# First expert's prompt rows by a selection product instead of a gather, its first low part on GpSimd, and two moved steps in attention

## The reference, cut to what matters

```
h2 = rms_norm(x, norm2_g)
aff = softmax(h2 @ w_router)                 # tokens x 16
gates, idx = top_k(aff.T, cap)               # each expert picks its tokens: 32 of the prompt, 64 of the sample
xe = h2[idx]
ye = (silu(xe @ w_gate) * (xe @ w_up)) @ w_down
x[idx] += ye * gates
```

## Time and profile before

| | us |
|---|---|
| median of 3 runs (1507.14 to 1507.4) | 1507.22 |
| the profiled execution, its own time | 1507.2 |
| its span | 1505.4 |
| TensorE busy | 1481.9 (98%) |
| VectorE busy | 1246.6 (83%) |
| ScalarE busy | 1115.2 (74%) |
| GpSimd busy | 285.9 (19%) |

### The profile page before, as it was taken

One profiled execution on the slowest core, in us unless ns is written; L12 is line 12 of the kernel. 1 busy time (PEld: TensorE's weight loads), 2 busy tenths in 40 slices (PEclk: granted clock), 3 DMA queues, 4 the chain that ended last, 5 costly groups with the idle time before them and its releaser, 6 DMA issues.

```text
span 1505.4 us, 18866 instructions
## 1 busy us (share of the span) xinstructions
PE 1481.9 (98%) x7283; PEld 1212.8 (81%) x7283; DVE 1246.6 (83%) x1237; ACT 1115.2 (74%) x1354; POOL 285.9 (19%) x115
## 2 busy tenths in 40 slices
PE   7999999999999999999999999999999999999997
PEld 6788887677778888888888888888888888888886
DVE  5358688875898989898988989898988989898985
ACT  7556476866487878878787878878787878878784
POOL 1012020000110404132240404132240404131010
PEclk9999999999999999999999999999999999999999
DMA  6111112204699999999999999999999999999993
GB/s 238 57 56 57 57 34 79 87 1 152 251 350 396 374 393 376 388 380 386 382 377 392 376 393 374 388 381 387 383 373 391 376 393 376 388 383 387 393 380 107
DMA packets 192105, 447.47 MB, mean 297 GB/s; under 512 B 13257, under 2 KB 13585, under 8 KB 192017
## 3 DMA queue, kind: packets, MB, share of 16 engines
q1 hardware_dynamic: 187632, 433.56, 77.4%
q0 software_dynamic: 4224, 12.65, 3.7%
q10 hardware_dynamic: 160, 0.07, 0.0%
HBM read 433.66 MB, written 12.58 MB: 296 GB/s over the span
## 4 chain that ended last, share of the span: by engine, by line
PE 95%; ACT 2%; DVE 2%; DMA 0%; issue 0%; POOLq 0%; POOL 0%; DVEq 0%; ACTq 0%
PE ps L1044 23%; PE ps L1046 23%; PE ps L1045 23%; PE ps L658 6%; PE ps L660 5%; PE ps L659 5%; PE ps L1108 1%; PE ps L896 1%; PE ps L932 1%; PE ps L1029 1%; PE ps L916 1%; ACT wih L1166 0%; PE ps L771 0%; ACT yr L1226 0%; PE ps L766 0%
## 5 line engine op out<-in xcount | busy, mean ns | idle before, releaser
L2039 DVE TENSOR_TENSOR wl<-raw,wh 128x2048 fp32r<-128x2048 f32 x384 | 872.1, 2289 | 114.7 <-ACT wh L1495 112.5
L1495 ACT CAST wh<-raw 128x2048 fp32r<-128x2048 f32 x384 | 729.7, 1915 | 117.5 <-PE ps L1046 116.2
L1044 PE MATMUL ps<-wh,XTh 128*128 128x512 f32 x1016 | 401.8, 395 | 0.6 <-DVE wl L2039 0.6
L1046 PE MATMUL ps<-wl,XTh 128*128 128x512 f32 x1016 | 396.3, 390 | 0.0
L1045 PE MATMUL ps<-wh,XTl 128*128 128x512 f32 x1016 | 395.4, 389 | 0.0
L1046 PEld LDWEIGHTS ps<-wl,XTh 128*128 128x128 f32 x1016 | 190.7, 188 | 40.9
L1044 PEld LDWEIGHTS ps<-wh,XTh 128*128 128x128 f32 x1016 | 190.8, 188 | 38.4 <-DVE wl L2039 1.0
L1045 PEld LDWEIGHTS ps<-wh,XTl 128*128 128x128 f32 x1016 | 191.0, 188 | 37.8
L1044 PE MATMUL ps<-wh,gTh 128*128 128x512 f32 x512 | 200.9, 392 | 0.0
L1046 PE MATMUL ps<-wl,gTh 128*128 128x512 f32 x512 | 199.4, 390 | 0.0
L1045 PE MATMUL ps<-wh,gTl 128*128 128x512 f32 x512 | 199.2, 389 | 0.0
(11 more groups left out here) (277 smaller groups left out, 1625.5 us busy)
## 6 DMA issues: line engine op xcount, KB each, us to landing
raw<-in_w_gate SPq DMA_DIRECT2D x128, 1024.0 KB, 11.2
raw<-in_w_up SPq DMA_DIRECT2D x128, 1024.0 KB, 11.2
raw<-in_w_down SPq DMA_DIRECT2D x128, 1024.0 KB, 11.5
slice_raw<-in_w_in SPq DMA_DIRECT2D x5, 2048.0 KB, 7.8
X<-in_x_sample SPq DMA_DIRECT2D x8, 512.0 KB, 6.5
slice_raw<-in_w_out SPq DMA_DIRECT2D x2, 2048.0 KB, 8.3
X<-in_x_prompt SPq DMA_DIRECT2D x4, 512.0 KB, 7.1
slice_raw<-in_w_in SPq DMA_DIRECT2D x4, 512.0 KB, 7.5
```

The lines of the kernel that those rows point to most:

```text
L1044: pe.matmul(out, hi, rhs_h, start=first, stop=False)
L1046: return pe.matmul(out, hi, rhs_l, start=False, stop=last)
L1495: act.copy(wh[:, n % CONV, :], raw[:, n % RAW, :]).then_inc(s_wh, 1)
L2039: dve.tensor_tensor(wl[:, n % CONV, :], raw[:, n % RAW, :], wh[:, n % CONV, :].bitcast(F32), ALU.subtract).then_inc(s_wl, 1)
```

## The change

In the attention loop, ScalarE's copy of the last value unit is done at step 4 instead of step 5, and from step 24 on TensorE's fillers come ahead of the transposes of mixed weights, as in the steps before.

Between router and first expert, the first expert's prompt rows are no longer gathered. VectorE writes the indices as numbers (`idxf`); TensorE multiplies them by a matrix with one row of ones (`pick`), which spreads the first expert's 32 indices over all partitions; VectorE compares them with each partition's token number (`token`, a new small input) and scales by the token's root (`onehot`, two tiles of 128 by 32); TensorE multiplies the residual rows `X` by that, two products for each of eight feature blocks, into the PSUM columns beside the turned sample rows. The sample rows alone are turned earlier, between the rounds. The fourth pair of feature blocks is done inside the first weight tile, whose order of products changes. The low part of weight tile 0 moves from VectorE to GpSimd, behind the gather of the sample rows. The copy of the candidates moves ahead of the second half of the prompt's softmax, and the sample's gates move behind the first of the four rounds. TensorE's busy-work is shortened.

```diff
+            sp.dma_start(token[:], a["token_index"]).then_inc(s_wr, 16)
...
             gather_sample(0)
+            pool.wait_ge(s_wh, 1)
+            pool.tensor_tensor(wl[:, 0, :], raw[:, 0, :], wh[:, 0, :].bitcast(F32), ALU.subtract).then_inc(s_wl, 1)
...
             pool.wait_ge(s_route, 2)
-            gather_prompt(0)
-            pool.memset(nlam[:, 1:2], 0.0).then_inc(s_issued, 1)
             gather(1)
...
-                if i < len(ATT):
-                    for x in FILL.get(i, ()):
-                        fill(x)
+                for x in FILL.get(i, ()):
+                    fill(x)
...
-                if i >= len(ATT):
-                    for x in FILL.get(i, ()):
-                        fill(x)
...
-                keep_busy(6)
+                keep_busy(6 if r < 3 else 3)
+            pe.wait_ge(s_gat, 16)
+            for k in range(KD):
+                pe.transpose(ps[:, pair_bank(k // 2), (k % 2) * CAP:(k % 2) * CAP + CAP_S],
+                             XE[0:CAP_S, k * P:(k + 1) * P], ident[0:CAP_S, 0:CAP_S])
             pe.wait_ge(s_top, (CAP_S + CAP_P) // 8)
-            keep_busy(14)
-            pe.wait_ge(s_tables, 1)
+            keep_busy(2)
+            pe.wait_ge(s_onehot, 1)
+            pe.matmul(ps[:, 2, 2 * P:2 * P + CAP_P], pick[0:GR, :], idxf[0:GR, :], start=True, stop=True).then_inc(s_topT, 1)
+            keep_busy(1)
+
+            def first_prompt_rows(j):
+                for k in (2 * j, 2 * j + 1):
+                    for t in range(2):
+                        mm = pe.matmul(ps[:, pair_bank(j), (k % 2) * CAP + CAP_S:(k % 2 + 1) * CAP],
+                                       X[:, t, k * P:(k + 1) * P], onehot[:, t, :], start=(t == 0), stop=(t == 1),
+                                       skip_group_check=True)
+                mm.then_inc(s_xtp0, 1)
...
-                    pe.wait_ge(s_wl, n + 1)
-                    for k in range(4):
...
+                    pe.wait_ge(s_wh, n + 1)
+                    for j in range(2):
+                        pe.wait_ge(s_xth0, j + 1)
+                        for k in (2 * j, 2 * j + 1):
+                            pe.matmul(out, XTh[0][:, k, :], h_[:, k, :], start=(k == 0), stop=False)
+                        if j == 0:
+                            first_prompt_rows(3)
+                        pe.wait_ge(s_xtl0, j + 1)
+                        for k in (2 * j, 2 * j + 1):
+                            pe.matmul(out, XTl[0][:, k, :], h_[:, k, :], start=False, stop=False)
+                    pe.wait_ge(s_wl, n + 1)
                     for k in range(4):
+                        mm = pe.matmul(out, XTh[0][:, k, :], l_[:, k, :], start=False, stop=False)
...
-            turn_first_rows()
-            pe.wait_ge(s_pad, 3)
+            pe.wait_ge(s_tables, 1)
+            pe.wait_ge(s_onehot, 3)
+            for j in range(3):
+                first_prompt_rows(j)
+            pe.wait_ge(s_pad, 2)
...
-                if i in (2, 5):
+                if i in (2, 4):
                     copy_unit("tok", len(SLICES) - 1, ORDER[4] if i == 2 else ORDER[5])
...
+            dve.wait_ge(s_topT, 1)
+            ch.mark(dve.tensor_copy(cand[0:CAP_S, :], ps[0:CAP_S, 3, 0:P]))
             affinity_scaled(prompt, stat_of[:, :, 2], 2)
...
-            dve.wait_ge(s_topT, 1)
-            ch.link(dve.tensor_copy(cand[0:n, :], ps[0:n, 3, 0:P]))
...
-            ch.mark(dve.tensor_tensor(gate[0:n, 0:NE], val[0:n, first], val[0:n, second], ALU.max))
...
                 top_eight(rest, c, ps[rest, 2, 0:2 * P] if c == 0 else aff[rest, :], CAP_S // 8 + c // 8 + 1, c + 8 < CAP_P)
+                if c == 0:
+                    ch.mark(dve.tensor_tensor(gate[0:n, 0:NE], val[0:n, first], val[0:n, second], ALU.max))
+            dve.tensor_copy(idxf[0:GR, :], topi[0:GR, 0:CAP_P]).then_inc(s_onehot, 1)
             dve.transpose(pidx[0:CAP_P, :], topi[rest, 0:CAP_P]).then_inc(s_route, 1)
             dve.transpose(gate[rest, :], topv[rest, 0:CAP_P]).then_inc(s_tables, 1)
+            dve.wait_ge(s_topT, 2)
+            for t in range(2):
+                dve.tensor_scalar(onehot[:, t, :], ps[:, 2, 2 * P:2 * P + CAP_P], token[:, t:t + 1],
+                                  roots2[:, root_place(t):root_place(t) + 1], ALU.is_equal, ALU.mult).then_inc(s_onehot, 1)
...
-            dve.wait_ge(s_issued, 1)
-            split(0)
             xt_first_copy()
+            dve.wait_ge(s_wl, 1)
             for n in range(1, AHEAD):
```

More of the change, by code:

```diff
@@ L262, in build @@
         cand = at("cand", 211360, [P, 2 * CAP_S])
+        pick = at("pick", 211872, [P, P])
+        onehot = at("onehot", 212384, [P, 2, CAP_P])
+        idxf = at("idxf", 212640, [P, CAP_P])
+        token = at("token", 212896, [P, 2])
         wout_low = slice_low
@@ L329, in build @@
         s_pad = sem("spare_columns_cleared")
-        s_issued = sem("first_gather_issued")
+        s_onehot = sem("first_prompt_indices_cast_then_one_hot_rows")
         s_tables = sem("gates_and_output_rows_ready")
@@ L587, in gather @@
                 if e == 1:
-                    pool.wait_ge(s_xtp0, 4)
+                    pool.wait_ge(s_xtp0, 1)
                 else:
@@ L1016, in _ @@
                 pe.wait_ge(s_top, CAP_S // 8 + r)
-                keep_busy(6)
-            pe.wait_ge(s_top, (CAP_S + CAP_P) // 8)
-            keep_busy(14)
-            pe.wait_ge(s_tables, 1)
+                keep_busy(6 if r < 3 else 3)
[3 more added lines that the diff above has]
+                             XE[0:CAP_S, k * P:(k + 1) * P], ident[0:CAP_S, 0:CAP_S])
+            pe.wait_ge(s_top, (CAP_S + CAP_P) // 8)
+            keep_busy(2)
[9 more added lines that the diff above has]
+                mm.then_inc(s_xtp0, 1)
             def turn_rows(e, half):
                 if half == 0:
-                    pe.wait_ge(s_gat, 32 * (e + 1))
+                    pe.wait_ge(s_gat, 32 * e + 16)
                 else:
@@ L1031, in turn_rows @@
                 mm.then_inc(s_xtp, 1)
[L1033 to L1039, removed]
             def products(out, parts, rhs_h, rhs_l, first, last):
@@ L1125, in _ @@
                 turns = q % NS == 1 and e + 1 < NE
+                if q == NS:
+                    pe.wait_ge(s_pad, 3)
                 if e >= 1 and q % NS == 0:
@@ L1869, in beside @@
                 if i == 13:
-                    dve.wait_ge(s_wr, 32)
+                    dve.wait_ge(s_wr, 48)
                     dve.memset(wr[:, :, NE:32], 0.0).then_inc(s_wrg, 1)
@@ L1927, in _ @@
             dve.memset(afft[:], 0.0).then_inc(s_clear, 1)
+            ch.mark(dve.memset(pick[0:GR, :], 0.0))
             dve.memset(tabf[:, 128:256], 0.0).then_inc(s_clear, 1)
@@ L1955, in _ @@
             h2_copied(2)
+            ch.own()
+            ch.mark(dve.memset(pick[CAP_S:CAP_S + 1, :], 1.0))
             gla_turned_low(1)
@@ L2115, in shape_constants @@
     return {"ident": np.eye(P, dtype=f), "rot": np.ascontiguousarray(rot), "scan_mask": scan,
-            "pair_mask": mask}
+            "pair_mask": mask, "token_index": np.arange(2 * P, dtype=f).reshape(2, P).T.copy()}
 def kernel(**inputs):
```

## The result

The changed kernel takes **1515.07 us** (median of 5 runs, 1514.04 to 1516.02) against 1507.4 (1507.14 to 1508.02) for the kernel before, run beside it: 1.005 times as long, 95% interval 1.0039 to 1.0061. So it is 7.7 us slower, where 1505.9 was forecast with a range up to 1507.9. The profiled execution is the longest of the five: 1516.02 us, span 1514.2.

A forecast was written before the change was run, and what follows sets the result against it. TensorE was taken as the bound (95% of the chain), so only its waits count: 1.3 and 0.2 gained in attention, 0.2 lost before the third tile, 1.3 off 1507.2, giving 1505.9 us, range 1504.4 to 1507.9.

The forecast's parts named there:

- Attention: Attention steps 4 and 24 to 26: shorter TensorE waits for ScalarE's copies save 1.3 and 0.2 us.
- The rounds: Prompt's search rounds: first starts at 404.23 instead of 404.62, second at 405.94; last search ends 0.2 us earlier.
- GpSimd's price: Weight tile 0's low part on GpSimd: 4.5 us, between 4.5 and 6.6, costing TensorE nothing.
- The margin: After the first round: VectorE's gates' operation starts 0.15 us before GpSimd's subtraction, in the same order each time.
- the rival: GpSimd starts before the gates' operation and holds VectorE until 410.4; 1509.9 us, or 1512.0; chance 13%.
- The hold: After the rounds: GpSimd holds VectorE's index cast until 410.5; bounds nothing and 0.55 us.
- From first maxima to prompt rows: Router stage: first round starts at 404.23, TensorE starts on the prompt rows at 411.45.
- 0.9 a pair: Prompt-row products on TensorE: each pair of feature blocks takes 0.9 us, three pairs lasting until 414.15.
- dear end of 1.5 a pair: Prompt-row products: upper bound of 1.5 us per pair, if weight loads don't overlap.
- VectorE's low part stays last: Before the third weight tile: TensorE's wait still ends on VectorE's low part; tile starts at 421.3, 0.2 us lost.
- The removed gather: First expert's prompt rows: product replaces gather, so TensorE starts on them at 411.45 instead of 413.63.

The follow-up runs named there:

- e2: The kernel before with only the two changed orders in attention (value copy at step 4, fillers first late on); 1506.15 us against 1507.32.
- e1: The changed kernel with more TensorE busy-work between the rounds and the prompt rows, filling its waits; 1512.18 us against 1507.32 for the kernel before.
- e5: e1 plus one busy-work product after each feature block of the first three pairs, the fourth pair's two blocks set apart; 1511.91 us.
- e6: e1 plus two busy-work products after each feature block of the first three pairs, the fourth pair's two blocks set apart; 1512.63 us.
- e7: The changed kernel with a 64th indirect transfer, a gather whose rows nobody uses; 1510.78 us against 1507.26 for the kernel before.
- e9: The kernel before, gather kept, plus attention orders, moved copy and gates, half of tile 0's low part on GpSimd, tile 1's low part earlier; 1505.42 us.
- e10: e1 with the gates' operation one round later, so that it falls into GpSimd's subtraction; 1517.52 us, one run.
- e3: The kernel before with only its TensorE busy-work shortened, in the last round and behind the rounds; 1508.34 us against 1507.32.
- e4: e1 with GpSimd's subtraction held back until the cast of the indices is done; 1511.69 us against 1507.32 for the kernel before.
- e12: The changed kernel with half the low part on GpSimd, waits filled, third and fourth pairs inside the first tile, low parts reordered, 64 transfers; 1505.43 us.
- e13: e9 with the gates' operation moved behind the transpose of the indices; 1504.84 us against 1507.3 for the kernel before.
- e14: e12 with the gates' operation behind the transpose of the indices and one busy-work product less behind the third round; 1505.77 us.

## Why the prediction was wrong, point by point

- **Attention: right in mechanism, 0.3 short.** 1.3 + 0.2 was forecast. `wT` is late next, as written (0.28 before L920), and the two waits shrink by 1.5, but in e2, with attention alone, 1.2 arrives at the first maxima.
- **The rounds: right.** From first to second maxima 1.72 us (406.20 - 404.48; forecast 405.94 - 404.23 = 1.71), later rounds 1.49.
- **GpSimd's price: right**, 4.60 for 4.5, though a straight line through the two rows shown gives 4.3. **The margin** of the gates' operation was 0.15, as forecast (406.00 against 406.15), and e1, e5, e6 and e7 have the same 0.15, so in the changed kernel the rival did not happen. The reason given for calling it safe ("the order is the same each time") fails in e9, a variant in which both start within a hundredth; e10 shows the rival's mechanism at 3.25 us.
- **The hold: right in kind, 0.5 too small.** The cast was to be held until 410.5; it ended at 411.29. It was let go not at the end of the subtraction (410.75) but 0.04 after the second of the two memsets behind it (411.25); in e1 likewise (410.92, 410.96). The two-input operation of e10, by contrast, was let go at the end of the subtraction, with the same two memsets still to come.
- **From first maxima to prompt rows: 0.76 late** (412.46 - 404.48 = 7.98 for 411.45 - 404.23 = 7.22), most of it the hold.
- **The step that failed: "0.9 a pair".** At full clock it was right (0.95 in e1). It was taken at full clock without asking what the thinned busy-work and the passes do to the clock; no term of the sum and no rival had it. A pair took 1.75 to 1.77 (5.30 by 3), a product of the tile 0.43 for 0.22, and the third tile came 7.06 later in the stage, not 0.6 (421.3 - 404.23 = 17.07 for 16.46). Of these 6.45 us, 0.76 lies before the prompt rows and 5.7 behind their start (428.00 - 412.46 = 15.54 for 421.3 - 411.45 = 9.85). The range's dear end of 1.5 a pair was for loads that don't overlap; the cause was another. Not all of it is the clock: e5's stage less its six products of busy-work (19.67 - 6 by 0.23) is 18.3, an estimate of this order of work at full clock, still 1.2 above the forecast.
- **"VectorE's low part stays last": wrong** at half clock: TensorE has no wait before the third tile. At full clock it is right (0.96 for `wl` in e5).
- **The removed gather: a second step that failed.** It was priced by the wait it ends; nothing was put down for a program with one transfer fewer, and the end grew by 2.0. That alone makes 1505.9 + 2.0 = 1507.9, the range's upper end.

## What to carry to other kernels

Busy-work ahead of a stage and a wait in that stage are one thing: before thinning the one or replacing the other by many small products, read the granted clock of that stretch and price everything behind it at both levels. Compare the last microseconds of the span as well, since a change at the start of a stage can lengthen the end. Where two instructions of different engines can hold each other, a margin of 0.15 us is thin: in e9 it was gone. Move the small one out of reach.

## What the runs showed of the hardware

- The clock fell behind 3.2 us of light work (two waits of 0.8 and 0.4 us, small transposes, three full products), and in e1 behind 2.84 us of plain-float passes with 32 columns though TensorE had no idle time at all. It stayed at half for 6.8 us in e1, e3 and e4, twice 6.8 in e10, and 13.7 in the changed kernel and e7; TensorE was busy for nearly all of that (5.2 of 6.8 in e3). In the profiles of e5 and e6 one or two full products of 0.23 us after every four passes kept it full.
- The same work does not bring the same clock in each execution. In e9, e12 and e13 the clock also fell at about 402.6, for 3.4 us, though TensorE was busy for 2.5 of the 3.6 us before that, as in e4 and e14, where it stayed full there. What decides between them stays open.
- With 63 indirect transfers GpSimd's closing drain ended 2.6 us after the output had landed, in all seven profiles with that count; with 64 (eight profiles) and 65 (one) 0.3 after.
- A cast of 0.18 us beside GpSimd took 1.12 to 1.14 and was held beyond the subtraction, over two memsets that followed it, in the changed kernel and in e1, e5, e6 and e7. A two-input operation was let go with the subtraction's end (e9, e10).
